# Two SSM read-out products for four, the fold on VectorE, and a re-ordered front and attention in a one-core kernel of a hybrid block

## What is computed

```python
proj = rms_norm(h, norm1_g) @ w_in                     # q 512, k 128, v 128, u 512 columns
attn = sliding_window_attention(q, k, v, ...)          # 8 heads, window 128, meta tokens and a sink
ssm  = s5_ssm(u, ...)                                  # 32 groups of 64 complex states
h = h + concatenate([rms_norm(attn), rms_norm(ssm)]) @ w_out
h = h + peer_ffn(rms_norm(h, norm2_g), ...)            # per token 8 x 16 experts, gathered rows
```

```python
bu_r, bu_i = einsum(u, bbar_r), einsum(u, bbar_i)      # bbar = coef * b, complex
s_r, s_i = scan(a_r, a_i, bu_r, bu_i)                  # s[t] = a * s[t-1] + bu[t], complex
y = einsum(s_r, c_re) - einsum(s_i, c_im) + d * u
z = gelu(y); z = z * sigmoid(z @ glu_w + glu_b)
```

## Time and profile before

| | |
|---|---|
| median of 3 executions | 1283.33 us (1281.91 to 1285.24) |
| the profiled execution | 1284.34 us, span 1282.6 us |
| busy in the span: PE, DVE, ACT, POOL | 1103.5, 758.7, 528.1, 319.8 us |
| first gather, last gather | 164.70 us, 975.93 us |
| DMA mean over the span | 308 GB/s |

### The profile page before, as it was taken

The page is one execution under the profiler, slowest core; times in us unless marked ns, Lnnn a source line. Parts: engine busy times, 40 slices in busy tenths (PEclk is TensorE's granted clock), DMA queues, the critical chain, the costliest instruction groups (busy, mean ns, idle before and its releaser), DMA issues.

```text
span 1282.6 us, 12167 instructions
## 1 busy us (share of the span) xinstructions
PE 1103.5 (86%) x3770; PEld 585.4 (46%) x3770; DVE 758.7 (59%) x1973; ACT 528.1 (41%) x1381; POOL 319.8 (25%) x302
## 2 busy tenths in 40 slices
PE   5998778888999979986898969898887899988998
PEld 5675534434444434432343434343432644543675
DVE  6564463469999666468775777785566322332343
ACT  4332226844344544344556463555463221212231
POOL 5100022244444333334232234333223000000000
PEclk9989889999999999999899999999898899999988
DMA  7021598789999999999999998999988454545430
GB/s 298 1 99 66 213 389 315 236 293 423 405 362 409 423 422 425 423 422 420 417 426 424 425 399 338 426 422 421 424 313 356 175 205 189 213 197 184 180 131 17
DMA packets 51728, 395.22 MB, mean 308 GB/s; under 512 B 5536, under 2 KB 10400, under 8 KB 11472
## 3 DMA queue, kind: packets, MB, share of 16 engines
q0 software_dynamic: 37536, 270.90, 52.3%
q1 hardware_dynamic: 13552, 122.83, 24.0%
q10 hardware_dynamic: 576, 0.72, 0.2%
HBM read 393.38 MB, written 1.05 MB: 308 GB/s over the span
## 4 chain that ended last, share of the span: by engine, by line
PE 52%; DVE 20%; DMA 12%; ACT 11%; issue 4%; POOL 0%; DVEq 0%; ACTq 0%
PE bank L1681 16%; PE bank L1374 12%; DMA expert_rows<-in_peer_uv,peer_idx 11%; DVE expert_rows L1320 8%; PE bank L1895 3%; PE bank L1928 2%; ACT L1442 2%; PE bank L1087 2%; ACT L1354 2%; PE bank L2079 1%; PE bank L1550 1%; ACT peer_diag L1361 1%; PE bank L1906 1%; PE bank L401 1%; PE bank L1588 1%
## 5 line engine op out<-in xcount | busy, mean ns | idle before, releaser
L1374 PE MATMUL bank<-expert_rows,peer_diag 128*128 128x512 f32 x896 | 452.3, 637 | 95.9 <-ACT peer_diag L1361 94.5
L1387 POOL DMA_INDIRECT expert_rows<-in_peer_uv,peer_idx x256 | 292.8, 1144 | 558.4 <-PE bank L1374 463.5
L1320 DVE CUSTOM_DVE_ANT_0 expert_rows<-expert_rows,HN 128x1024 f32<-128x1024 f32 x256 | 308.8, 1221 | 85.6 <-DMA expert_rows<-in_peer_uv,peer_idx 84.7
L1374 PEld LDWEIGHTS bank<-expert_rows,peer_diag 128*128 128x128 f32 x896 | 168.3, 199 | 311.8 <-issue 159.8
L1681 PE MATMUL bank<-w_ring,b_xt 128*128 128x512 f32 (+1 forms) x576 | 276.7, 604 | 14.0 <-ACT b_sq L1710 11.6
L1354 ACT ACTIVATE peer_dots<-peer_dots 128x1 f32<-128x1 f32 x256 | 51.6, 202 | 302.4 <-DVE peer_dots L1320 301.8
L1681 PEld LDWEIGHTS bank<-w_ring,b_xt 128*128 128x128 f32 x576 | 104.9, 196 | 118.0 <-issue 113.0
L1361 ACT ACTIVATE peer_diag<-ident,peer_dots 128x128 f32<-128x128 f32 x224 | 89.9, 402 | 7.3
L1355 ACT ACTIVATE peer_dots<-peer_dots,peer_ex 128x1 f32<-128x1 f32 x256 | 75.4, 295 | 8.3
L1442 ACT ACT_TABLE_LOAD x53 | 68.0, 1283 | 15.8 <-PE bank L1011 6.2
L2388 POOL DMA_DIRECT2D out<-x_res x4 | 2.2, 559 | 276.9 <-DVE x_res L1608 164.3
(11 more groups left out here) (355 smaller groups left out, 1284.8 us busy)
## 6 DMA issues: line engine op xcount, KB each, us to landing
w_ring<-in_w_in_e SPq DMA_DIRECT2D x16, 2048.0 KB
w_ring<-in_w_in_o SPq DMA_DIRECT2D x14, 2048.0 KB
w_ring<-in_w_query SPq DMA_DIRECT2D x8, 2048.0 KB
w_ring<-in_w_out SPq DMA_DIRECT2D x4, 2048.0 KB
w_ring<-in_w_out_e SPq DMA_DIRECT2D x4, 2048.0 KB
w_ring<-in_w_out_o SPq DMA_DIRECT2D x4, 2048.0 KB
w_ring<-in_w_in SPq DMA_DIRECT2D x2, 2048.0 KB
expert_rows<-in_peer_uv,peer_idx POOLq DMA_INDIRECT x256, 13.3
```

The lines of the kernel that those rows point to most:

```text
L1320: t.dve.tensor_tensor_reduce(u, u, t.HN[:, it // PH, :], 1.0, 0.0, ALU.mult, ALU.add, self.dots[:, it, k:k + 1]).then_inc(*self.dotted.add())
L1374: ins = t.pe.matmul(t.PS[2 * T + c][:, :], self.diag[:, d % self.RD, :], self.slot(n)[:, D + c * 512:D + (c + 1) * 512], start=k == 0, sto ...
L1387: t.pool.indirect_dma_start(self.slot(n), None, t.dram["peer_uv"], bass.IndirectOffsetOnAxis(ap=self.idx[:, it, k:k + 1], axis=0)).then_in ...
```

## The change

1. **Read-out of tile 0.** `turn_back` adds up two pairs of `g4` on DVE (L937, L938 of the changed kernel), so that `out` issues the products with `cpr` and `cni` alone. Tile 1 keeps four.
2. **Tables.** The fold and the second half of the angles move from POOL to DVE, as generators (`fold`, `angles(1)`); an Abs on ACT becomes the fourth DVE operation of the angles.
3. **Order of the front.** The fold and `norm1(1)` run beside `project_u`; `angles(1)` and `last_sines` beside `project_qkv(0)`; `head_norm1(1)` beside `mix_attention(0)`, in the banks 0 and 1, waiting for `attn_ready[0]` instead of `half_added[0]`. The mixer gets 1.0 steps for each SSM step.
4. **Attention of tile 1.** It has two banks for its turns, and every part but the scores one step later; normalisation yields once more.
5. **Experts.** PE's expert products and POOL's gathers first wait for `heads_ready[1]`.
6. **Projections.** In `project`, ACT yields `L.lead` steps ahead of each evacuation, and `inherit` hands a bank of lane 0 to lane 1 as its spare, once lane 0 is finished; that is so at lane 1's odd layer, not at its even one.

```diff
@@ -291,6 +291,8 @@
         if T == 1:
+            for _ in range(3):
+                yield
             t.pe.wait_ge(*t.u_ready.at(4))
@@ -432,6 +437,7 @@
+    banks = ((t.PS[2], t.PS[3]), (t.PS[0], t.PS[1]))[T]
@@ -488,17 +494,17 @@
-            t.pe.wait_ge(*t.half_added[0])
+            t.pe.wait_ge(*t.attn_ready[0])
@@ -522,7 +528,9 @@
-    turn_bank, out, apt = t.PS[2], t.PS[3], t.apt[T]
+    turn_banks, out, apt = ((t.PS[2],), (t.PS[2], t.PS[6]))[T], t.PS[3], t.apt[T]
+    TB = len(turn_banks)
+    sums, exps, turns, places, mixes = ((0, 1, 2, 3, 4), (1, 2, 3, 4, 5))[T]
@@ -543,13 +551,14 @@
-            if i >= 1:
-                t.pe.wait_ge(*placed.at(i))
+            if i >= TB:
+                t.pe.wait_ge(*placed.at(i - TB + 1))
@@ -565,13 +574,13 @@
-        for i in range(NU + 4):
+        for i in range(NU + mixes):
...
-            if i >= 4:
-                mix(i - 4)
-            if 2 <= i <= NU + 1:
-                turn(i - 2)
+            if i >= mixes:
+                mix(i - mixes)
+            if turns <= i < NU + turns:
+                turn(i - turns)
@@ -696,8 +706,8 @@
-        t.diagonal, t.folded, t.sines = self.dts.at(3), self.folded.at(1), [self.sines.at(2), self.sines.at(3)]
+        t.diagonal, t.folded, t.sines = self.dts.at(3), self.turns.at(4), [self.sines.at(2), self.sines.at(3)]
@@ -729,15 +739,22 @@
-    def angles(self):
+    def angles(self, half):
...
-        h = slice(0, self.HALF)
+        h = slice(half * self.HALF, (half + 1) * self.HALF)
...
-        ch.step(t.dve.tensor_tensor(S, bc(self.frac[:, h], SPAN + 1), bm(t.col("time"), self.HALF), ALU.mult))
-        ch.step(t.dve.tensor_scalar(C, S, ROUND, ROUND, ALU.add, ALU.subtract))
-        ch.step(t.dve.tensor_tensor(S, S, C, ALU.subtract))
+        ch.mark(t.dve.tensor_tensor(S, bc(self.frac[:, h], SPAN + 1), bm(t.col("time"), self.HALF), ALU.mult))
+        yield
+        ch.wait()
+        ch.mark(t.dve.tensor_scalar(C, S, ROUND, ROUND, ALU.add, ALU.subtract))
+        yield
+        ch.wait()
+        ch.mark(t.dve.tensor_tensor(S, S, C, ALU.subtract))
+        yield
+        ch.wait()
...
+        yield
@@ -759,11 +776,9 @@
-        t.act.wait_ge(*self.folded.at(2))
+        t.act.wait_ge(*self.turns.at(5))
...
-        h = slice(self.HALF, ST)
-        t.ach.step(t.act.activation(t.COS[:, h, :], t.SIN[:, h, :], ACT.Abs))
-        self.sine(h)
+        self.sine(slice(self.HALF, ST))
@@ -782,27 +797,23 @@
-        t.dve.tensor_scalar(self.nfi, self.cfi, -1.0, None, ALU.mult).then_inc(*self.turns.add())
-    def pool(self):
-        t, ch = self.t, self.t.pch
+        ch.step(t.dve.tensor_scalar(self.nfi, self.cfi, -1.0, None, ALU.mult))
+    def fold(self):
+        t, ch = self.t, self.t.dch
...
-        t.pool.wait_ge(*self.turns.at(4))
-        t.pool.wait_ge(t.late, 64)
-        ch.mark(t.pool.tensor_tensor(t.cpr[:, :, :], t.cr[:, :, :], bc(self.cfr, w), ALU.mult))
-        ch.mark(t.pool.tensor_tensor(t.ct[:, :, :], t.ci[:, :, :], bc(self.cfi, w), ALU.mult))
-        ch.mark(t.pool.tensor_tensor(t.cni[:, :, :], t.cr[:, :, :], bc(self.nfi, w), ALU.mult))
+        t.dve.wait_ge(t.late, 64)
+        ch.mark(t.dve.tensor_tensor(t.cpr[:, :, :], t.cr[:, :, :], bc(self.cfr, w), ALU.mult))
+        ch.step(t.dve.tensor_tensor(t.ct[:, :, :], t.ci[:, :, :], bc(self.cfi, w), ALU.mult))
+        ch.mark(t.dve.tensor_tensor(t.cni[:, :, :], t.cr[:, :, :], bc(self.nfi, w), ALU.mult))
+        yield
...
-        ch.step(t.pool.tensor_tensor(t.cnr[:, :, :], t.ct[:, :, :], t.cpr[:, :, :], ALU.subtract))
-        ch.step(t.pool.tensor_tensor(t.cpr[:, :, :], t.cpr[:, :, :], t.ct[:, :, :], ALU.subtract))
-        ch.step(t.pool.tensor_tensor(t.ct[:, :, :], t.ci[:, :, :], bc(self.cfr, w), ALU.mult))
-        t.pool.tensor_tensor(t.cni[:, :, :], t.cni[:, :, :], t.ct[:, :, :], ALU.subtract).then_inc(*self.folded.add())
-        h = slice(self.HALF, ST)
-        S, C = t.SIN[:, h, :], t.COS[:, h, :]
-        ch.step(t.pool.tensor_tensor(S, bc(self.frac[:, h], SPAN + 1), bm(t.col("time"), self.HALF), ALU.mult))
-        ch.step(t.pool.tensor_scalar(C, S, ROUND, ROUND, ALU.add, ALU.subtract))
-        t.pool.tensor_tensor(S, S, C, ALU.subtract).then_inc(*self.folded.add())
+        ch.step(t.dve.tensor_tensor(t.cpr[:, :, :], t.cpr[:, :, :], t.ct[:, :, :], ALU.subtract))
+        ch.mark(t.dve.tensor_scalar(t.cnr[:, :, :], t.cpr[:, :, :], -1.0, None, ALU.mult))
+        ch.step(t.dve.tensor_tensor(t.ct[:, :, :], t.ci[:, :, :], bc(self.cfr, w), ALU.mult))
+        t.dve.tensor_tensor(t.cni[:, :, :], t.cni[:, :, :], t.ct[:, :, :], ALU.subtract).then_inc(*self.turns.add())
+        yield
@@ -851,9 +862,10 @@
             t.pe.wait_ge(*back.at(j + 1))
-            for n, (x, c) in enumerate(((0, t.cpr), (1, t.cni), (2, t.cni), (3, t.cnr))):
+            parts = ((0, t.cpr), (1, t.cni), (2, t.cni), (3, t.cnr))[0:2 + 2 * T]
+            for n, (x, c) in enumerate(parts):
                 ins = t.pe.matmul(y[a][32 * r:32 * r + 32, :], c[:, j, :], t.g4[:, j % 2, x, :],
-                                  start=False, stop=n == 3, skip_group_check=True)
+                                  start=False, stop=n == len(parts) - 1, skip_group_check=True)
             ins.then_inc(*read.add())
@@ -917,6 +929,13 @@
                                           bm(tab[:, j, off:W], 2), ALU.mult)
+                if T == 0:
+                    t.dch.mark(ins)
+            if T == 0:
+                g = t.g4[:, j % 2]
+                t.dch.wait()
+                t.dve.tensor_tensor(g[:, 0, :], g[:, 0, :], g[:, 3, :], ALU.subtract)
+                ins = t.dve.tensor_tensor(g[:, 1, :], g[:, 1, :], g[:, 2, :], ALU.add)
             ins.then_inc(*back.add())
@@ -1365,6 +1384,7 @@
         N = self.NI * TOPK
+        t.pe.wait_ge(*t.heads_ready[1])
         for n in range(-1, N):
@@ -1693,6 +1713,8 @@
                 continue
+            for _ in range(L.lead):
+                yield
             ps = banks[j % nb]
@@ -1800,6 +1822,12 @@
+def inherit(L):
+    if L.T == 1 and L.spare is None and "finished" in L.other.done:
+        L.spare, L.free[1] = L.other.pt, L.other.done["x"]
@@ -2282,6 +2310,7 @@
     outs = [(hd(L.mixed[:, 0:512]), (), None), (L.o3[:, 0:4, :], (), None), (L.o3[:, 4:8, :], (), None)]
+    inherit(L)
     yield from turn_x(L, "ln_e")
@@ -2468,24 +2498,25 @@
-    tables.angles()
+    run(tables.angles(0))
...
-    tables.pool()
...
-    mixer = one_by_one(lambda: inputs, lambda: side_by_side(norm1(t, 1), project_qkv(t, 0)), tables.last_sines,
+    mixer = one_by_one(lambda: side_by_side(inputs, tables.fold(), norm1(t, 1)),
+                       lambda: side_by_side(project_qkv(t, 0), one_by_one(lambda: tables.angles(1), tables.last_sines)),
...
-                       lambda: side_by_side(attention1(t, 0), project_qkv(t, 1)), lambda: mix_attention(t, 0))
+                       lambda: side_by_side(attention1(t, 0), project_qkv(t, 1)),
+                       lambda: side_by_side(mix_attention(t, 0), head_norm1(t, 1)))
...
-    run(beside(ssm(t, 0), mixer, 0.8))
+    run(beside(ssm(t, 0), mixer, 1.0))
...
-    run(side_by_side(close_mixer(t, 0), head_norm1(t, 1)))
+    run(close_mixer(t, 0))
@@ -2495,6 +2526,7 @@
     t.w.pump(t.sp)
+    t.pool.wait_ge(*t.heads_ready[1])
     peer.gathers(0, peer.FEW)
```

More of the change, by code:

```diff
@@ L303, in dve @@
     def dve():
+        if T == 1:
+            for _ in range(3):
+                yield
         t.dve.wait_ge(t.constants, 32)
@@ L496, in pe @@
         for g in range(2):
[L497 removed]
+            ins = t.pe.transpose(banks[1][:, g * P:(g + 1) * P], t.kx[:, g].rearrange("p x d -> p (x d)"), t.ident[:, :])
         if T == 0:
@@ L580, in dve @@
             t.dch.step(t.dve.tensor_scalar(t.nsink[:, :], t.row("sinks"), -1.0, None, ALU.mult))
-        for i in range(NU + 4):
-            if i < NU:
-                t.dve.wait_ge(*scored.at(i + 1))
-                if i >= R:
-                    t.dve.wait_ge(*turned.at(i - R + 1))
-                for e, h in enumerate(sets[i]):
-                    ins = t.dve.tensor_tensor_reduce(p_at(i, e), s_at(i, e), bias, 1.0, t.nsink[:, h:h + 1], ALU.add,
+        for i in range(NU + mixes):
+            n = i - sums
+            if 0 <= n < NU:
+                t.dve.wait_ge(*scored.at(n + 1))
+                if n >= R:
+                    t.dve.wait_ge(*turned.at(n - R + 1))
+                for e, h in enumerate(sets[n]):
+                    ins = t.dve.tensor_tensor_reduce(p_at(n, e), s_at(n, e), bias, 1.0, t.nsink[:, h:h + 1], ALU.add,
                                                      ALU.min, t.amn[:, h:h + 1])
                 ins.then_inc(*least.add())
-            if i == NU:
+            if n == NU:
                 t.dve.wait_ge(*least.at(NU))
                 t.dve.tensor_tensor(t.adsk[:, :], t.amn[:, :], t.nsink[:, :], ALU.subtract).then_inc(*sunk.add())
-            if i == NU + 3:
+            if i == NU + mixes - 1:
```

(7 more changed lines are left out.)

26 lines of the change are left out of this document (14 added, 12 removed).

## The result

The changed kernel takes 1253.36 us, median of 4 executions (1249.07 to 1255.81), against 1284.28 (1281.91 to 1285.79) for the kernel before: a ratio of 0.9757, 95% interval 0.9726 to 0.9789. The profiled execution, the fastest of the four, has a span of 1247.3 us.

The account below looks back on a forecast made before the run. TensorE binds 34 to 109 us, ACT tile 1's attention, DMA rate 300 to 900 us. 1284.34 - 10.6 + 0 - 3.0 - 6.2 = 1264.5, less 1.0 for the median: 1263.5 us; own range 1256 to 1270, wider 1254 to 1276.

Parts of the forecast that it names:

- Lead: Lane 0's projections: ACT's evacuation three lane steps later fills DMA dips in 900-960 us; -3.0 us, ends -6.1 and +3.
- Front: Stretch up to the first gather: TensorE's path shortens, then DVE binds; -10.6 us, first gather at about 154 us.
- (e): Behind the last g: read-out 0.5 us shorter, gelu table load gone or hidden -1.3, PE's wait at L493 gone -1.9.
- (f): PE in 90 to 117 us gets new gaps, which slow the rows behind them: +1.4 us.
- Rival B: PE's gaps in the DVE-bound stretch bring the clock to half level, 1.2 GHz: 1268.7 us; chance 0.13.
- (a): Tile 1's norm1 beside project_u removes PE's 3.99 us wait for HN: -4.0 us, least -2.5 if a uT wait comes.
- (b): Read-out of a state tile on PE 0.50 us shorter for each of 16 j: 8.0 us, counting only where PE binds.
- Term (c): PE's wait for the glu_w DMA at 73.33 us, 2.2, and slow rows behind it, 3.0: -5.2 us, least -2.0.
- Rival A: In 20 to 109 us DVE's added work is in series with PE's, not beside it: slower, 1288.7 us; chance 0.06.
- E: Rival for the tail: spare bank doesn't help, ACT's passes matching PE's products, or isn't taken: 1269.7 us; chance 0.04.
- C: Rival on tile 1's attention: its two more steps, 9.2 us, end last before gather 32: 1272.7 us; chance 0.10.
- D: Rival: DMA dips close wholly (-3.1), clock holds (-1.4), DVE overlaps PE better by 3 us: 1256 us; chance 0.08.

## Why the prediction was wrong

The direction was right, and the range was missed by 0.6 us at its low end. By steps:

**Lead, the step that failed: -3.0 forecast, -16.8 (12 to 22) alone and -14.6 when taken out.** The mechanism was right and its size was not. I priced it by one window of lost transfer rate, 900 to 960 us, and halved it for no measured reason. That window did fill, from 370 to 413 GB/s with the lead alone, which is the whole 6.2 us. Read over 700 to 960 us (398 and 411 GB/s) the same rule gives 8.2. The larger price stood in a view that I had read for PE only: ACT's own waits for PE's bank, 48 us in the expert phase, each with expert work behind it. They don't all count, and how many of them the DMA covers was not measured, but their sum bounds the gain, which the end of -6.1 did not.

**Front: -10.6 forecast, -4.6 (1.3 to 7.8) in time, -5.8 at the first gather.** Followed through the two traces, attention 0 ends 1.4 us later than forecast. From there to the last g it takes 30.8 us for 27.0: DVE waits 5.3 us for L664 and not 1.6, because the first group takes 6.72 us and not 3.70. Behind the last g, up to mT's end, 0.5 us went of the 1.8 forecast: the table load is gone, as (e) had it, but the gate products stand at the low level (2.08 us) and the last sigmoids take 1.14 us, for 0.62 before. Behind mT 2.2 us went for 1.9. So the step of the front that failed is (f): it had +1.4 for the clock, and the L664 group alone took 3.0.

Rival B described this (half level in the DVE-bound stretch, 5 us) and had 0.13, but it counted 2.1 us for a slow L1003, which the kernel before pays already. With the clock held by fillers the first gather is at 153.3, near the forecast of 154, in part by luck: that run is rid of those 2.1 us, which the forecast left in, and its last g still ends at 120.9 and not at 117.4. The Trainium skill, page "TensorE: Matmul & The Clock Gate", section "HAM oscillation — how this bites in real kernels", says that TensorE is throttled again when it waits between bursts of matmuls. The traces agree in direction: 0.69 of full with waits between the products, 1.00 with the waits filled. But it does not happen at every wait: behind the 2.2 us for glu_w the products were slow in three of five profiles.

(a): the wait for HN went, but up to 2.3 us of waiting for uT came in the seven profiles of the changed front, 2.0 in the profiled execution of the changed kernel, so that -2.0 was left there, less than the term's end of -2.5. (b) counted for nothing in either kernel. Its 8 us of PE were bought with additions on DVE that bind next, and with gaps on PE. For the 1.6 us of waiting for L653 the prediction reads the groups at 118.5 and 119.5; they stand at 114.86 and 119.48, and 118.49 is a read-out.

**Term (c), -5.2.** The wait went. The slow rows behind it were priced at 3.0 and cost 3.2 where they occur, but they were taken from one profile, and two of five profiles of the same code don't have them.

**Order and the tables on DVE: right.** The cycle is 3.30 us, and the 9.7 us of the tables are covered (the run with them on POOL is not to be told from the changed kernel). The additions' 8.8 us were costed at nothing too, and that was wrong for those behind attention 0: without them the first gather is 5.2 us earlier, clock included. From close_mixer to query 1.9 was forecast and 2.2 measured (mT's end to the first gather 32.2 before, 30.0 after).

**Attention of tile 1: 0 forecast, not told from 0 in time.** The step of 4.62 us stayed, as said.

**Spare bank: -6.2 forecast,** -11.4 (7.8 to 15.0) alone, +8.1 when taken out, 7.7 and 5.0 in the traces. The four waits went. The mechanism was right and the size 2 to 5 us too small by ratio.

**Rival A** (DVE in series) is refuted: first gather before 164, faster. **E** and **C** as well. **D** came nearest in time (1256), with 0.08; only its part on the DMA is in the runs, at more than its 3.1 us.

**Signs.** One sign of being wrong came true: the last g ends at 122.6 and was to be before 122. DVE is busy for 18.9 of the 25 us before it, 75% and not over 90. The other did not: from first to last gather it is shorter. DMA in 850 to 950 us (1.01) and the waits for b_sq in the tail are as forecast.

The lead was under by 12 to 14 us and the bank by 2 to 5, the front over by 6: with these signs the total missed by 11. That it missed by no more is luck: the front's error hid a part of the other two.

## What to carry to other kernels

An in-order engine that waits on one stream holds up the other stream behind it: before pricing an edit that moves such a wait, list that engine's own waits by what ended them, over the whole phase, and take their sum as the bound (48 us here, of which 16.8 came). Taking work from an engine that then waits for another was worth nothing here, and on TensorE the gaps went with a lower clock; try thrown-away products in the gap before shortening it. A price read from slow rows of a single profile needs a second profile of the same code.

## What was not expected of the hardware

The granted clock differs between executions of one program at the same place: 0.90 and 1.00 from 75 to 109 us with equal queues and an equal 2.2 us wait ahead. That is 3.2 of the 7.0 us between the first gathers of these two profiles. In the profiles where the first gather was 6 to 7 us earlier, 1.9 to 2.3 of it were left at gather 208, so it hardly shows in the total. Fillers of 0.46 us in waits of 1.4 to 3.0 us kept the clock at 1.00 from 109 to 131 us, where it had been 0.69.
